# Tail of the routing reordered, spare products in TensorE's pauses, two weight parts sent later

## The reference

```python
gp = softmax(x @ w_group_router + b_group_router)         # 4 groups, top 1
el = (x @ w_expert_router + b_expert_router)              # 8 experts in that group, top 2
...
for e in range(N_EXPERTS):
    hdn = jax.nn.silu(x @ w_gate[e]) * (x @ w_up[e])      # 1024 -> 256
    y = y + combine[:, e:e + 1] * (hdn @ w_down[e])       # 256 -> 1024
x = h + y
```

## Time and profile before

| | us |
|---|---|
| median of 3 runs | 614.64 (614.0 to 615.8) |
| the profiled execution, its own time | 614.34 |
| its span, first to last instruction | 612.7 |
| TensorE matmul busy | 532.0 (87%) |
| TensorE weight loads busy | 391.5 (64%) |
| VectorE, ScalarE, GpSimd busy | 218.6, 169.6, 139.4 |
| DMA | 140.80 MB, mean 230 GB/s |

### The profile page before, as it was taken

One profiled execution on the slowest core, in us unless ns is written; L12 is line 12 of the kernel. 1 busy time (PEld: TensorE's weight loads), 2 busy tenths in 40 slices (PEclk: granted clock), 3 DMA queues, 4 the chain that ended last, 5 costly groups with the idle time before them and its releaser, 6 DMA issues.

```text
span 612.7 us, 9450 instructions
## 1 busy us (share of the span) xinstructions
PE 532.0 (87%) x3252; PEld 391.5 (64%) x3253; DVE 218.6 (36%) x602; ACT 169.6 (28%) x421; POOL 139.4 (23%) x230
## 2 busy tenths in 40 slices
PE   4899999999989999999956976899938779999984
PEld 4788988987558668888854633566624555556651
DVE  4753244333667755347671121111101111121111
ACT  6833343332443332135431111111111111111110
POOL 0132232222503200015525012122201122222212
PEclk9999999999999999999966999999959989999998
DMA  8741000012313101299894299999999999999993
GB/s 315 294 108 36 13 23 1 24 46 76 116 57 104 34 35 36 60 409 420 317 355 190 95 318 376 371 374 395 378 375 404 372 382 387 375 358 370 383 339 71
DMA packets 33445, 140.80 MB, mean 230 GB/s; under 512 B 10488, under 2 KB 11147, under 8 KB 21350
## 3 DMA queue, kind: packets, MB, share of 16 engines
q1 hardware_dynamic: 25776, 124.33, 52.4%
q0 software_dynamic: 5856, 12.60, 8.5%
q10 hardware_dynamic: 1766, 3.25, 1.6%
HBM read 131.15 MB, written 16.46 MB: 241 GB/s over the span
## 4 chain that ended last, share of the span: by engine, by line
DMA 26%; PE 22%; DVE 4%; issue 3%; ACT 1%; POOL 1%; DVEq 0%; POOLq 0%; ACTq 0%; SPq 0%
PE ps L847 11%; DMA expert_w<-in_w_gate 11%; DMA expert_w<-in_w_up 9%; PE ps L863 5%; DMA token_gates<-gate_rows 2%; DMA more_rows<-token_rows,idx_now 2%; DMA g_rows<-token_rows,idx_all 1%; DMA token_rows<-h_sb 1%; PE ps L506 1%; PE ps L507 1%; PE ps L511 1%; PE ps L765 1%; DVE xT L1490 1%; PE ps L834 1%; ACT s_act L1134 1%
## 5 line engine op out<-in xcount | busy, mean ns | idle before, releaser
L847 PE MATMUL ps<-expert_w,xT 128*64 128x256 f32 x1152 | 134.1, 390 | 12.9 <-issue 5.1
L847 PEld LDWEIGHTS ps<-expert_w,xT 128*64 128x64 f32 x1152 | 98.6, 141 | 52.1 <-issue 22.2
L863 PE MATMUL ps<-expert_w,hT 128*64 128x512 f32 x272 | 63.9, 611 | 18.0 <-DVE hT L1508 16.8
L1664 POOL DMA_INDIRECT out<-y_sb,idx_now x17 | 27.2, 1602 | 175.9 <-issue 128.2
L1501 DVE SCALAR_TENSOR_TENSOR hid<-s_act,gate,ps 128x256 f32<-128x256 f32 x18 | 12.0, 666 | 139.5 <-ACT s_act L1134 139.5
L863 PEld LDWEIGHTS ps<-expert_w,hT 128*64 128x64 f32 x272 | 21.9, 140 | 49.2 <-issue 42.9
L1134 ACT ACTIVATE s_act<-ps,gate 128x256 f32<-128x256 f32 x18 | 8.5, 474 | 131.2 <-PE ps L847 131.2
L506 PE MATMUL ps<-w_in_hi,aT_hi 128*128 128x384 f32 (+2 forms) x120 | 43.7, 369 | 0.0
L507 PE MATMUL ps<-w_in_lo,aT_hi 128*128 128x384 f32 (+2 forms) x120 | 40.8, 345 | 0.0
L1513 DVE COPY y_sb<-ps 128x512 f32<-128x512 f32 x18 | 12.4, 692 | 74.1 <-PE ps L863 68.4
L1139 ACT ACTIVATE y_sb<-ps 128x512 f32<-128x512 f32 x18 | 10.8, 597 | 78.8 <-PE ps L863 73.2
(11 more groups left out here) (227 smaller groups left out, 924.6 us busy)
## 6 DMA issues: line engine op xcount, KB each, us to landing
expert_w<-in_w_gate SPq DMA_DIRECT2D x32, 1024.0 KB, 9.2
expert_w<-in_w_up SPq DMA_DIRECT2D x32, 1024.0 KB, 9.5
expert_w<-in_w_down SPq DMA_DIRECT2D x30, 1024.0 KB, 9.5
w_in_raw<-in_w_in SPq DMA_DIRECT2D x8, 608.0 KB, 10.4
w_out_raw<-in_w_out SPq DMA_DIRECT2D x8, 512.0 KB, 3.8
token_rows<-h_sb ACTq DMA_DIRECT2D x6, 512.0 KB, 8.3
out<-h_sb SPq DMA_DIRECT2D x6, 512.0 KB, 11.5
x_sb<-in_x_prompt SPq DMA_DIRECT2D x4, 512.0 KB, 12.7
```

The source lines that it names most:

```text
L847: mm = pe.matmul(ps[r, GU_BANK[q.o], g * FH:(g + 1) * FH], xT[:, q.o, k, r], w_gu(b, lane, k, g), start=(k == 0), stop=(k == KD - 1))
L863: mm = pe.matmul(ps[r, 4 + half, :], hT[:, q.o, k, r], w_dn(b, lane, k, half), start=(k == 0), stop=(k == 1))
L1664: pool.indirect_dma_start(out=out, out_offset=bass.IndirectOffsetOnAxis(ap=idx, axis=0), in_=y_sb[:, buf, :], in_offset=None, compute_op=A ...
```

## The change

In TensorE's queue: `slots(1)` and `ranks(4)` go ahead of `logits(5, 1)`, `slots(2)` and `slots(3)` too; `more_slots(1..3)` no longer wait for `idx_done` and go ahead of `ranks(5)`; the last tile's slot product is cut in two (`last_slots`), the 32 columns of token numbers first, the 64 of factors behind VectorE's reading of the first; `more_slots(4)` and `(5)` stay behind. `keep_clock` runs products of bf16 constants into PSUM bank 3, which nothing reads: 8 ahead of `ranks(5)` and 40 ahead of the wait for the first gather. In VectorE's queue `route_weights(5)` goes from ahead of `slot_of(5)` to behind the copy of `idx_all`. In SP's queue the two down parts of pair 2 wait until the gather of pair 0 has landed. Nothing else is changed.

```diff
--- before.py
+++ after.py
@@ -445,7 +445,9 @@
                 store_h(i)
             sp.wait_ge(o_mm, 2 * NT)
             store_h(NT - 1)
-            load_pair(sp, 2, 2)
+            load_pair(sp, 2, 2, range(4))
+            sp.wait_ge(main.gathered[0], 16)
+            load_pair(sp, 2, 2, range(4, 6))
             sp.wait_ge(counts_done, 1)
 
             more = sp.alloc_register("more_total")
@@ -774,24 +776,38 @@
                 pe.matmul(ps[:, 6, 0:E], ones_bf, m_sum[:, 0, :], start=True, stop=False)
                 pe.matmul(ps[:, 6, 0:E], ltri_bf, m_sum[:, 1, :], start=False, stop=True).then_inc(rank_mm, 1)
 
+            def slot_product(i, at, block, cols, last):
+
+                for c in range(2):
+                    mm = pe.matmul(ps[:, 5, at + cols.start * E:at + cols.stop * E], slot_a[:, i % SLOT_BUFS, 2 * block + c, :],
+                                   slot_b[:, i % SLOT_BUFS, c, cols, :].rearrange("t n e -> t (n e)"),
+                                   start=(i == 0 and block == 0 and c == 0), stop=(last and c == 1), skip_group_check=True)
+                return mm
+
             def slots(i):
 
                 pe.wait_ge(slot_a_done, 2 * i + 1)
                 pe.wait_ge(slot_b_done, 2 * (i + 1))
-                for c in range(2):
-                    mm = pe.matmul(ps[:, 5, 0:3 * E], slot_a[:, i % SLOT_BUFS, c, :], slot_b[:, i % SLOT_BUFS, c, :, :].rearrange("t n e -> t (n e)"),
-                                   start=(i == 0 and c == 0), stop=(i == NT - 1 and c == 1), skip_group_check=True)
-                mm.then_inc(slot_mm, 1)
+                slot_product(i, 0, 0, slice(0, 3), False).then_inc(slot_mm, 1)
+
+            def last_slots():
+
+                pe.wait_ge(slot_a_done, 2 * NT - 1)
+                pe.wait_ge(slot_b_done, 2 * NT - 1)
+                slot_product(NT - 1, 0, 0, slice(0, 1), False).then_inc(slot_mm, 1)
+                pe.wait_ge(idx_done, 2)
+                pe.wait_ge(slot_b_done, 2 * NT)
+                slot_product(NT - 1, 0, 0, slice(1, 3), True).then_inc(slot_mm, 1)
 
             def more_slots(i):
 
                 pe.wait_ge(slot_a_done, 2 * (i + 1))
-                if i == 1:
-                    pe.wait_ge(idx_done, 5)
-                for c in range(2):
-                    mm = pe.matmul(ps[:, 5, 128:128 + 3 * E], slot_a[:, i % SLOT_BUFS, 2 + c, :], slot_b[:, i % SLOT_BUFS, c, :, :].rearrange("t n e -> t (n e)"),
-                                   start=False, stop=(i == NT - 1 and c == 1), skip_group_check=True)
-                mm.then_inc(more_mm, 1)
+                slot_product(i, 128, 1, slice(0, 3), i == NT - 1).then_inc(more_mm, 1)
+
+            def keep_clock(n):
+
+                for _ in range(n):
+                    pe.matmul(ps[:, 3, 0:P], ones_bf, ltri_bf, start=True, stop=True)
 
             for i in range(NT):
                 out_part(i, 0, 0)
@@ -812,16 +828,24 @@
             last = NT - 1
             logits(last, 0)
             h_transposes(last, 1)
+            slots(1)
+            ranks(last - 1)
+            slots(2)
+            slots(3)
             logits(last, 1)
-            ranks(last - 1)
-            for i in range(1, last):
-                slots(i)
+            slots(last - 1)
+            for i in range(1, last - 1):
+                more_slots(i)
+            pe.wait_ge(h_done, 2 * NT)
+            keep_clock(8)
             ranks(last)
-            slots(last)
+            last_slots()
             pe.wait_ge(pos_done, NT)
             pe.matmul(ps[:, 6, 128:128 + E], ones_bf, m_sum[:, 0, :], start=True, stop=True).then_inc(total_mm, 1)
-            for i in range(1, NT):
-                more_slots(i)
+            pe.wait_ge(idx_done, 5)
+            more_slots(last - 1)
+            more_slots(last)
+            keep_clock(40)
 
 
             pe.wait_ge(counts_done, 1)
@@ -1439,7 +1463,6 @@
             table_place(NT - 2)
             route(NT - 1)
             route_experts(NT - 1)
-            route_weights(NT - 1)
             slot_of(NT - 1)
             dve.wait_ge(slot_mm, NT)
 
@@ -1457,7 +1480,9 @@
                                     ).then_inc(idx_done, 1)
 
             slot_tokens(0, idx_all)
+            route_weights(NT - 1)
             table_place(NT - 1)
+            dve.wait_ge(slot_mm, NT + 1)
             slot_factors(0, gate_all)
             dve.tensor_copy(idx_all[:, PAIRS:], no_token).then_inc(idx_done, 1)
```

## The result

The changed kernel takes 628.57 us, median of four runs (627.04 to 631.43); four runs of the kernel before, on the same chip and in turn with them, have a median of 614.32 (613.38 to 615.8). The ratio is 1.023, with a 95% interval of 1.019 to 1.028: 14 us slower, where 7 us faster was forecast. The profiled execution took 631.43 us, its span is 629.8.

What follows compares the result with a forecast made beforehand. A saturated expert-weight stream, held until TensorE reads pair 0's gate weights, bounds the kernel. Earlier transposes 3.45, their full clock 0.64 and `gate_up` 2.79 sum to 6.9 us: 614.34 to 607.4, median 607.7; range 605.0 to 611.2.

Steps and rivals of the forecast that it cites:

- the stream with it: Expert weight stream: an earlier first refill, 348.40 to 341.5, moves the whole saturated stream, so the end comes 6.9 us earlier.
- the stream that eats the gain: Rival, no change: the 246 us weight stream takes 3% longer and eats the 7 us; chance 0.04.
- gather landed: First gather of `g_rows`: issued at 317.9, landing taken at 324.0, within bounds of 322.3 and 326.7.
- transposes start, behind the products: TensorE's transposes start when the spare products end, at 325.3 instead of 328.75: 3.45 us gained.
- first refill: SP's first weight refill, after TensorE has read pair 0's gate weights: from 348.40 to 341.5 us.
- The order of ranks, slots and weights: Routing tail of the last tile: 0.95 from ranks, 0.5 from later `route_weights`, 0.6 from the split product; gather issued 2.1 earlier.
- The hold: SP's queue: holding two down parts leaves 2 MB fewer competing with the first gather, so it lands at 324.0.
- holding back buys nothing: Rival on the held down parts: gather lands at 326.7, gain only 5.5 us, 609.2 us; chance 0.12.
- The fillers: 40 spare TensorE products behind more_slots: 0.11 then 0.06 us each, ending at 325.3, raising the clock for transposes and `gate_up`.
- the forecast's 2.79 us: `gate_up` of pair 0 at full clock: 7.06 us to its last read instead of 9.85.
- The sum: Tail up to the end of pair 0's `gate_up`: 3.45 + 0.64 + 2.79 = 6.9 us earlier.
- worth its full time: Everything ahead of the first refill at 348.40 us counts fully, as an earlier refill moves the saturated stream as a whole.

Runs made afterwards that it cites:

- e7: The kernel before with only SP's new wait, holding back the two down parts of pair 2 until the first gather has landed: 611.70 us, ratio 0.993.
- e2: The changed kernel with 151 more do-nothing waits in TensorE's queue, so its loop begins 256 places later than in the kernel before: 610.87 us, ratio 0.993.
- e3: The changed kernel without its 48 spare products, loop 9 places behind that of the kernel before: 610.89 us, ratio 0.993.
- e5: The changed kernel with its 48 narrow products replaced by 6 fp32 products of 423 columns, loop moved 33 places: 610.94 us, ratio 0.993.
- e8: The kernel before with only five wide fp32 products ahead of the wait for the first gather, loop moved 20 places: 611.14 us, ratio 0.994.
- e6: As e5, but SP sends all six parts of pair 2 without waiting for the gather: 613.06 us, ratio 0.996.
- e4: As e2, but SP sends all six parts of pair 2 without waiting for the gather: 613.96 us, ratio 0.998.
- e10: The changed kernel with 20 instead of 40 spare products behind more_slots, loop moved 65 places: 640.78 us, ratio 1.043.
- e1: The kernel before with 105 more do-nothing instructions in TensorE's queue, moving its loop as far as the change does: 634.93 us, ratio 1.032.

## Why the prediction was wrong

The step that failed is the one in which the products, as work in a pause, cost nothing but their own time, and "the stream with it": the same 264 us behind the refill. I counted the added instructions as time on the engine and as entries in queues, never as places of code. That place turned 264.3 us into 285.8: the loop (by the count above across 8 blocks of code instead of 7) was fetched again in each later turn, a mechanism that none of the prediction's rivals has. The nearest of them, the stream that eats the gain, names the wrong side: the stream kept its lead (its last issue is at 583.41, before at 589.30), and TensorE's code came late.

The steps ahead of it, with 1.66 us set off for the late start:

| step | forecast | measured |
|---|---|---|
| `idx_all` starts | 316.35 | 316.3 |
| gather issued | 317.9 | 317.8 |
| gather landed | 324.0 | 324.6 |
| transposes start, behind the products | 325.3 | 326.2 |
| `gate_up` of pair 0 | 7.06 us, full clock | 7.13 with the overlap of 0.07, full clock |
| first refill | 341.5 | 342.35 |

- *The order of ranks, slots and weights* came out as worked out: 2.1 us on the gather's issue.
- *The hold.* The gather took 6.8 us against 6.1 forecast and 8.76 before (4.7 in e7, with the hold alone): the mechanism was right, as the landings with and without it show. The rival, that holding back buys nothing, is out.
- *The fillers* took 0.11 us each in the profile after, all 40 of them; the forecast had the last ones at 0.06. The clock rose only behind them, and they end 0.9 us late. In e2 the same 40 took 3.39 us, so some ran at full clock. What they were for, `gate_up` at full clock, they did. But the forecast's 2.79 us for it is the difference from the 9.85 of before. With the gather early and no products at all, `gate_up` takes 8.8 (8.81 in e3, 8.82 in e7), so that full clock brings 1.7, and part of that pays for the products' own late end.
- *The sum.* 6.05 us in the changed kernel, 7.05 in e2 (refill less last store of `h_sb`: 41.65 us before, 34.6 in e2), against 6.9 forecast.

So the tail's account closes in size, but not all of it reaches the end, as the prediction took for granted ("worth its full time"): with its loop in place, and 151 idle instructions, the whole change is worth 4.2 us (e2). Of the whole, each kernel's gain by its ratio (good to some 2 us) stands against what its tail is shorter by: e3 4.2 of 4.7, e5 4.5 of 5.0, e7 4.1 of 5.2, e8 3.6 of 2.2, e6 2.2 of 4.2, but e2 4.2 of 7.1 and e4 0.9 of 4.8. Of the kernels whose loop fits, the last two alone carry 151 idle instructions; yet the last store of `h_sb` stands at 308.05 us in e4's profile and at 308.41 in that of the changed kernel, which has none, so I can't say that they are the cause. Between e5 and e6 it is the first pass over pairs 1 and 2 that the profile points to. TensorE's timeline of e5:

```profile
364.90 7.08 PE L871 MATMUL ps<-expert_w,xT 128*64 128x256 f32 x46 [4.29 <-issue]
...
381.10 8.81 PE L871 MATMUL ps<-expert_w,xT 128*64 128x256 f32 x64 [2.82 <-issue]
```

These waits for code, 4.3 and 2.8 us, are in a stretch where SP's next refill depends on what TensorE has read. But from the refill to the end the one profile of each kernel whose loop fits gives anything from 261 to 269 us, and e6 with the code of e5 the 261. Differences of 3 us can't be traced to a row in that spread; they stay open.

## What to carry to other kernels

Before adding instructions to an engine that later runs a long unrolled loop, read the code queue's packets and the pauses put down to "issue", before and after: if packets now come in turns that had none, it is the place of the loop, and moving it (by instructions that do nothing, or by fewer and wider products) is the test and the cure. A spare product costs instructions, not only time: six wide products kept the clock as 48 narrow ones did (`gate_up` at 7.13 us in e5 and in the changed kernel), with 24 instructions for 96. The best kernels here, e2, e3 and e5, at 610.9 us against 614.3 to 615.4 before, are equal, and the simplest of them is the change without its spare products.

## What the runs showed of the hardware

- A loop of 1,705 TensorE instructions ran four turns on one load of its code at five places and was fetched again in each later turn at three. Against e2, whose loop stays, this costs the changed kernel 18 us and e10, with fewer products, 30. The period is 256 instructions, as far as 0 and 256 against 105 and 206 show it.
- With the DMA engines saturated most of the packets cost nothing: some nine come in each later turn of the changed kernel, and two or three pauses. A pause inside a turn is of 0.3 to 2.8 us in the changed kernel and e1, one where the loop jumps back of 4.9 to 6.1, up to 11 in e10. Behind the jumps the granted clock is at half for a while, which makes the next `gate_up` 1.4 to 2.8 us longer.
- Between 170 and 180 us seven of the twelve profiles, that of the changed kernel among them, have a granted clock of 0.83; the others have 1.00. The last store of `h_sb` comes at 307.45 to 310.61 us in the seven, and at 305.14 to 306.75 in the five. The kernel before has 1.00 and e7, with the same code for TensorE up to there, 0.83, so this is an accident of the execution; it is why times of day in two profiles are compared here only from a common mark.
